# Where the last table's pieces and the token sums stand in the second layer's feed-forward queue

## What is computed

```python
mod = jax.nn.silu(c) @ w_ada + b_ada
sh1, sc1, gt1, sh2, sc2, gt2 = [m[:, None, :] for m in jnp.split(mod, N_MOD, axis=-1)]
...
x = x + gt1 * _rmsnorm(mixed @ w_out, g_post_mix)
h = _rmsnorm(x, g_pre_ffn) * (1.0 + sc2) + sh2
f = (jax.nn.silu(h @ w_gate) * (h @ w_up)) @ w_down
return x + gt2 * _rmsnorm(f, g_post_ffn)
```

## Time and profile before

| | us |
|---|---|
| median of 3 runs | 849.33 |
| lowest, highest | 847.21, 850.21 |
| the profiled execution | 848.88 |
| its span, first to last instruction | 847.1 |

### The profile page before, as it was taken

One profiled execution on the slowest core, in us unless ns is written; L12 is line 12 of the kernel. 1 busy time (PEld: TensorE's weight loads), 2 busy tenths in 40 slices (PEclk: granted clock), 3 DMA queues, 4 the chain that ended last, 5 costly groups with the idle time before them and its releaser, 6 DMA issues.

```text
span 847.1 us, 11576 instructions
## 1 busy us (share of the span) xinstructions
PE 832.3 (98%) x4131; PEld 689.5 (81%) x4131; DVE 690.0 (81%) x1180; ACT 458.5 (54%) x732; POOL 121.3 (14%) x92
## 2 busy tenths in 40 slices
PE   8999999999999999999999999999999999999897
PEld 5877888888888888888888788888888878778685
DVE  5898889888788776786789899898778878989973
ACT  5665555555657334533575655555575644554442
POOL 5500300302220021120420040040040000000300
PEclk9999999999999999999999999999999999999999
DMA  8996666575418888787428756666542577083431
GB/s 343 402 370 229 222 256 254 199 275 211 150 51 303 295 289 325 240 328 277 171 95 335 261 199 251 246 243 229 199 150 100 222 301 280 17 327 144 179 145 50
DMA packets 34795, 194.09 MB, mean 229 GB/s; under 512 B 4273, under 2 KB 4529, under 8 KB 17714
## 3 DMA queue, kind: packets, MB, share of 16 engines
q1 hardware_dynamic: 33410, 189.64, 60.1%
q0 software_dynamic: 1328, 3.71, 1.2%
HBM read 192.29 MB, written 1.05 MB: 228 GB/s over the span
## 4 chain that ended last, share of the span: by engine, by line
PE 83%; DVE 7%; DMA 5%; issue 2%; ACT 2%; SPq 1%; DVEq 0%; ACTq 0%
PE ps L1735 22%; PE ps L1737 22%; PE ps L1736 22%; PE ps L1848 4%; DMA wide_t<-scale_first 3%; DVE w_lo L1156 3%; DMA raw<-w_stream 2%; ACT w_hi L769 2%; PE ps L1912 2%; PE ps L2154 1%; PE ps L1772 1%; PE ps L1773 1%; PE ps L1779 1%; PE ps L1933 1%; PE ps L1934 1%
## 5 line engine op out<-in xcount | busy, mean ns | idle before, releaser
L1156 DVE TENSOR_TENSOR w_lo<-raw,w_hi 128x2048 fp32r<-128x2048 f32 (+2 forms) x126 | 286.5, 2279 | 57.2 <-ACT w_hi L769 56.1
L1735 PE MATMUL ps<-w_hi,t_hi 128*128 128x512 f32 (+2 forms) x712 | 282.0, 396 | 1.7 <-DVE w_lo L1156 0.9
L1737 PE MATMUL ps<-w_hi,t_lo 128*128 128x512 f32 (+2 forms) x712 | 275.1, 386 | 0.0
L1736 PE MATMUL ps<-w_lo,t_hi 128*128 128x512 f32 (+2 forms) x712 | 274.5, 385 | 0.0
L769 ACT ACTIVATE w_hi<-raw 128x2048 fp32r<-128x2048 f32 (+2 forms) x128 | 240.6, 1883 | 40.6 <-DMA raw<-w_stream 34.4
L666 POOL PARTITION_ALL_REDUCE wide_t<-wide_t x20 | 80.0, 3999 | 556.5 <-DVE wide_t L1282 555.5
L1735 PEld LDWEIGHTS ps<-w_hi,t_hi 128*128 128x128 f32 x712 | 133.8, 188 | 30.3 <-DVE w_lo L1156 2.9
L1737 PEld LDWEIGHTS ps<-w_hi,t_lo 128*128 128x128 f32 x712 | 133.7, 188 | 27.8
L1736 PEld LDWEIGHTS ps<-w_lo,t_hi 128*128 128x128 f32 x712 | 134.0, 188 | 25.2
L1282 DVE SCALAR_TENSOR_TENSOR wide_t<-ada,cs,wide_t 128x1024 f32<-128x1024 f32 x80 | 110.2, 1377 | 2.0 <-DMA ada<-w_ada 1.7
L1735 PE MATMUL ps<-w_hi,m_hi 128*128 128x512 f32 x208 | 84.3, 405 | 0.0
(11 more groups left out here) (257 smaller groups left out, 1078.4 us busy)
## 6 DMA issues: line engine op xcount, KB each, us to landing
raw<-w_stream SPq DMA_DIRECT2D x124, 1024.0 KB, 5.3
ada<-w_ada SPq DMA_DIRECT2D x80, 512.0 KB, 5.7
wide_t<-gains POOLq DMA_DIRECT2D x7, 512.0 KB, 4.8
mixed<-w_stream SPq DMA_DIRECT2D x3, 1024.0 KB, 7.6
raw<-w_stream SPq DMA_DIRECT2D x4, 656.0 KB, 6.9
mixed<-scale_first SPq DMA_DIRECT2D x2, 1024.0 KB, 10.4
wide_t<-shift_first SPq DMA_DIRECT2D x4, 512.0 KB, 11.1
wide_t<-scale_first SPq DMA_DIRECT2D x2, 1024.0 KB, 12.7
```

The lines of the kernel that those rows point to most:

```text
L1156: nc.vector.tensor_tensor(w_lo[:, U % RING, a:n], src[:, a:n], w_hi[:, U % RING, a:n].bitcast(F32), ALU.subtract).then_inc(s_lo, 1)
L1735: nc.tensor.matmul(dst, hi, w_h, start=first, stop=False)
L1736: nc.tensor.matmul(dst, hi, w_l, start=False, stop=False)
L1737: return nc.tensor.matmul(dst, lo, w_h, start=False, stop=last)
```

## The change

Five things: the eight pieces of layer 1's last table come as 2, 2, 3 in steps 0 to 2 and one in the second pair, in place of 1, 3, 1, 1, 1 in steps 0 to 4 and one in step 7; its table is made after step 10 and no longer in the second pair. `add_tokens` has two parts: the first three instructions come one step earlier, the last two stay. In a pair the third sum out of PSUM stands in front of a low part. `gated` waits for the table by its semaphore.

```diff
@@ def ffn_pieces(l)
-    return (1, 3, 1, 1, 1, 0, 0, 1, 0, 0, 0), (8,)
+    return (2, 2, 3, 0, 0, 0, 0, 0, 1, 0, 0), (10,)
...
-            def add_tokens(l):
+            def add_tokens(l, part):
 
                 upper, lower = slice(0, 4), slice(4, KT)
                 one, two = slice(0, P), slice(P, 2 * P)
+                if part:
+                    link(nc.vector.scalar_tensor_tensor(out=sums[:, upper, one], in0=sums[:, lower, two], scalar=-1.0,
+                                                        in1=sums[:, upper, one], op0=ALU.mult, op1=ALU.subtract))
+                    nc.vector.scalar_tensor_tensor(out=sums[:, lower, one], in0=sums[:, lower, one], scalar=-1.0,
+                                                   in1=sums[:, upper, one], op0=ALU.mult, op1=ALU.subtract).then_inc(s_sums, 1)
+                    return
                 dve.wait_ge(s_act_lo, l * N_SPLIT + turn_no("h2", 3))
                 link(nc.vector.tensor_tensor(sums[:, :, :], t_hi[:, :, :].bitcast(F32), t_lo[:, :, :].bitcast(F32), ALU.add))
                 link(nc.vector.tensor_tensor(sums[:, lower, two], sums[:, lower, two], sums[:, upper, two], ALU.subtract))
                 link(nc.vector.tensor_tensor(sums[:, upper, two], sums[:, upper, one], sums[:, upper, two], ALU.subtract))
-                link(nc.vector.scalar_tensor_tensor(out=sums[:, upper, one], ...
-                nc.vector.scalar_tensor_tensor(out=sums[:, lower, one], ...
...
                 add_products(l, j, twin_b, twin_a, PTB, 1, 2)
+                add_products(l, j, twin_b, twin_b, OUT, 4, 3)
                 split_lo(l, behind[2])
-                add_products(l, j, twin_b, twin_b, OUT, 4, 3)
                 split_lo(l, behind[3])
...
                 dve.wait_ge(s_sq, squares(n, 0))
+                dve.wait_ge(s_table, 4 * l + (1 if mid else 3))
                 gate_part(l, t, 0, 512)
...
                         if t == 0 and j == sums_step(l):
-                            add_tokens(l)
+                            add_tokens(l, 1)
+                        elif t == 0 and j == sums_step(l) - 1:
+                            add_tokens(l, 0)
                         elif t == 0 and j == sums_step(l) + 1:
                             sums_low(l)
```

More of the change, by code:

```diff
@@ L1191, in add_tokens @@
                 link(nc.vector.tensor_tensor(sums[:, upper, two], sums[:, upper, one], sums[:, upper, two], ALU.subtract))
[L1192 to L1195, removed]
             def sums_low(l):
```

## The result

The changed kernel takes 850.18 us in the median (849.0 to 851.92, 20 runs); the kernel before, beside it on the same chips, 848.73 us (846.7 to 850.8, 20 runs). The ratio is 1.0019 with a 95% interval of 1.001 to 1.0027: slower, by 1.5 us. The forecast was a gain of 0.66 us, written as 848.7 against the 849.33 us of the first three runs of before; against the 848.73 of the twenty it would be 848.1, so the miss is 2.1 us in the difference. The profiled execution of the changed kernel takes 849.34 us, its span 847.6, against 848.88 and 847.1 before: in this one pair of executions the difference is only 0.46 us.

What follows compares the result with a forecast made beforehand. TensorE was taken as the bound, by its idle times and clock. Against the profiled 848.88 us, -7.54 + 3.78 + 1.60 + 1.40 + 0.10 = -0.66 gave 848.2, or 848.7 from the 849.33 median; range 845.0 to 851.0.

Steps and rivals of the forecast that it cites:

- layer 0's stray sums: Layer 0, step 10: three sum instructions nobody needs, held beside GpSimd's reduction, make TensorE wait; loss 1.40 us.
- "cost nothing" for the third sum ahead of the low part: Layer 1's pairs: the sum in front brings the first pair's seventh product forward, gain 0.99 us; the delayed low part costs nothing.
- rival (e): First pair: the third sum's new place does nothing, VectorE being early without the early piece; same time, within the forecast's 0.50.
- The clock behind step 1's gap: Layer 1, step 1: TensorE's clock falls behind the new idle time; loss 1.60 us, between 0 and 1.7.
- The gap in step 1: Layer 1: three sum instructions between the gate products delay the second one and TensorE waits; loss 3.78 us.
- Rival (b): Layer 1, step 1: no new gap, the second gate product not being wanted so early; 843.3 us, chance 0.08.
- The second pair: Layer 1, steps 8 and 9: the sixth product's wait and the clock loss behind it go; gain 4.46 us.
- rival (d): Second pair stays late, by a weight load or ScalarE in place of GpSimd; 853.2 us, chance 0.07.
- The turns of steps 2 and 4: Layer 1: TensorE's waits at these turns for the second gate product go; gains 1.28 and 0.81 us.
- The table: Layer 1's last border: the last table, made later, delays the border's first instruction a little; loss 0.10 us.
- Rival (c): Layer 1's last border: the table is late; 849.2 us, or 850.2 if the reduction is held up; chance 0.08.
- Rival (a): New idle times are cheaper: no clock fall in step 1, or layer 0's sums slip between holds; 845.7 to 847.3, chance 0.27.

Runs made afterwards that it cites:

- E9: The changed kernel itself run again, on one chip beside the two fillings of its idle times one at a time: 850.1 us, ratio 1.0023.
- E1: The changed kernel without the three stray sum instructions in layer 0: 847.74 us, ratio 0.9993.
- E7: E2 with the third sum put back behind the low part, in both pairs: 841.76 us, ratio 0.9923.
- E5: The kernel before with only the three stray sum instructions added in layer 0's step 9, where no reduction runs: 848.34 us, ratio 1.0003.
- E6: The kernel before with only layer 1's last piece moved, and its reduction and the wait for the table with it: 844.22 us, ratio 0.995.
- E10: The changed kernel with 15 matmuls nobody reads filling only the idle time in layer 1's step 1: 848.25 us, ratio 0.9997.
- E2: E1 with the first three sum instructions of layer 1 behind both gate products of step 1 instead of between them: 842.54 us, ratio 0.993.
- E8: The changed kernel with all five sum instructions in layer 1's step 2, none in step 1 or layer 0: 844.57 us, ratio 0.9949.
- E12: The kernel before with only the third sum put ahead of the low part, in both pairs: 847.91 us, ratio 0.9997.
- E4: The kernel before with only the three stray sum instructions added in layer 0's step 10, between the gate products: 851.74 us, ratio 1.0035.
- E3: The changed kernel with both new idle times filled by matmuls nobody reads, 15 in layer 1's step 1 and 7 in layer 0: 847.85 us, ratio 0.9992.

## Why the prediction was wrong

The four old waits, the two new ones and their places were right. The sign was not: gains of 7.54 us and losses of 6.88 were to differ by 0.66, and three terms of the losses were too low, by 0.65 to 0.75 us each. What follows is read against E9's profile, which lies at the median. Its last matmul ends 1.23 us later than before, where the forecast was 0.66 us earlier. A term is the growth of the distance between two matmuls, one on each side of the place.

- **The step that failed first: layer 0's stray sums.** Forecast 1.40, measured 2.1 in both profiles, and 2.2 by E1 against the change. That the sums would be held beside GpSimd was right. I counted 1.0 of one hold and 2.0 of the other, and the two are there: 3.35 - 2.29 = 1.06 and 2.62 - 0.69 = 1.93. But there is a third one, 2.24 - 1.52 = 0.72, on the low part that the sums had pushed beside GpSimd's copy behind the reduction. It is the whole difference. I had closed the account at the end of the reduction, and did not ask what GpSimd does next and what the late queue would meet there.
- **The step that failed second: "cost nothing" for the third sum ahead of the low part.** Forecast 0.99 of gain; the seventh product comes 0.91 us earlier, 1.05 with the first distance behind it. But rival (e) was right, the missing piece does it alone, as E7 shows: the gain came out for a cause that was not mine. And behind the pairs 0.31 and 0.37 us are lost that I had put at nothing. For the second pair E7 and the other traces show that it is the order; behind the first, E5 and E6 lose 0.90 and 0.32 us without it, so there the cause is not shown. I had looked at who reads the low part, and not at VectorE's own queue, which stands idle 1.29 us for TensorE's fifth product with the low part behind it.
- **The clock behind step 1's gap.** Forecast 1.60; 1.50 to 1.58 in three profiles, 2.27 in E9's, and 2.2 by the ratios of E9 and E10. The size was right for the first profile and 0.67 too low for E9's, which lies above my bound of 1.7 too. Why the clock stays low longer in some executions is open.
- **The gap in step 1.** Forecast 3.78, measured 3.86 and 3.93. Step and size right, and E2 shows that the place between the gate products is the cause. Rival (b) is refuted. With the gap's clock it is 5.2 us by E2 against E1, more than what the split of the sums gives in a good place (E8 against E2, 1.6).
- **The second pair.** Forecast 4.46; 4.58 in E9's trace, 4.2 by E6's ratio. Right, and rival (d) refuted. The cause is the reduction, moved by the last piece alone.
- **The turns of steps 2 and 4.** Forecast 1.28 and 0.81; 1.27 and 0.77 in E9's trace. But the wait in step 2 is not in every execution of before: E12 has the same queue there, and TensorE turns all four at 695.27 without a wait; in E4 it is gone too. So of the 1.28 only a part counts in the median.
- **The table.** Forecast 0.10; the border waits for ScalarE, and E6's end loses nothing. Rival (c) refuted.

Sum of the differences in E9's trace: 0.73 (layer 0) + 0.68 (behind the pairs) + 0.67 (clock) + 0.15 (gap) - 0.10 (table) - 0.24 (all else) = 1.89 = 1.23 + 0.66. In the first profile, where the clock cost what I had said, the first two terms (0.74 + 0.64) alone turn the forecast gain of 0.66 into a loss; with the rest it is the 0.46 us seen there. Rival (a), to which I gave 0.27, said that the new idle times would be cheaper; layer 0's and the gap came out dearer, the clock as forecast or dearer. The changed kernel's first profile (+0.46) fell on an execution with the cheap form of the clock's loss; E9's, at the median, has the dear one.

The Trainium skill (GPSIMD Engine Reference, section Specifications) holds that VectorE's instructions with two SBUF inputs contend with GpSimd. The measured rows agree: the held instructions above all read two SBUF operands, and E5 has the same three sums at 2.29, 0.69 and 0.69 us. They also show that VectorE is not always the one held. In the changed kernel's profile a low part begins at 819.77, just ahead of the moved reduction, and takes its usual 2.28 us; the first half of the reduction then takes 5.20, where that of the one at 158.18 takes 3.23.

What stays open: before has executions with a mean clock of 1.0 that are no faster than those at 0.997 (848.55 and 849.01 among them), so part of its spread is not the clock; and I did not look for why some waits (step 2's turn, step 7's low part of the products, the one in layer 1's mixing part) stand in some profiles of a queue and not in others.

## What to carry to other kernels

Before work is put between two instructions of a queue, look up what is waiting for the second one: the same three instructions cost 5.2 us between the gate products and no wait behind them. When a condition like "the step before" is written for one case, ask which steps of the other cases meet it; here it woke 3.7 us of dead work in layer 0, which cost 2.2 us because GpSimd worked beside it. And when a queue is made later, follow it on, past the one reader of what was moved: one of my low terms lay in GpSimd's next instruction behind the reduction, the other in VectorE's own queue behind the low part.

## What the runs showed of the hardware

- In layer 0's step 10 three VectorE instructions with two SBUF inputs were held: two beside a reduction on GpSimd, by 1.06 and 1.93 us, and one beside its copy of 1.12 us, by 0.72. A sum that began 0.48 us ahead of the copy ran at its usual 0.69 us. The reduction took 8.60 us there and 7.68 in before: either engine can be the one held.
- TensorE's clock fell from 1.0 to 0.50, from 2.4 to 1.2 GHz, behind idle times of 3.67 us (in all four profiles that have it unfilled), 2.69 (in before, E4 and E12, not in E5) and 1.77 (in E4, not in the change, E9 or E10), and did not behind 2.38 us in E8. The same gap of 3.67 us cost 1.50, 1.56 and 1.58 us of clock in three executions and 2.27 in a fourth. With matmuls that nobody reads in the gap of step 1 the clock stayed at 1.0 behind it (profiles of E3 and E10).
